# Query tiles outside, head pairs inside: the pair order of the odd mixer's sparse attention

## The chip, the core and the metric

One core of a Trainium2 chip runs one program: two transformer blocks of depth two, one after the other, in float32. The metric is the device time of one execution in microseconds. TensorE is called PE, VectorE DVE, ScalarE ACT, GpSimd POOL, SyncE SP, as in the profile.

## The reference, cut to what matters

The second block's odd layer has a mixer with eight query heads in two key groups over 512 tokens. Each head attends three times: to 31 compressed keys, to selected blocks of 64 keys, and to a window of 512 keys. With 512 tokens, 16 blocks are selected out of 8, and the window covers everything, so both large branches are plain causal attention with their own keys and values. Cut to its core:

```python
def masked_softmax(s, mask):
    return jax.nn.softmax(jnp.where(mask, s.astype(jnp.float32), NEG_INF), axis=-1)
...
        o_sel = jnp.einsum('bgmqkl,bgqkld->bgmqd', p, vs)
...
        s = jnp.einsum('bgmqd,bgsd->bgmqs', qb, kwb)
        o_win = jnp.einsum('bgmqs,bgsd->bgmqd', masked_softmax(s, win_ok).astype(vwb.dtype), vwb)
        o = jnp.stack([o_cmp, o_sel, o_win], axis=-1).reshape(b, NSA_HEADS, Q_BLOCK, d, 3)
        return jnp.einsum('bhqdc,bhqc->bqhd', o, gb)
```

After it the mixer computes a retention over the same tokens, from columns of the same input projection, and an output projection of both.

## The kernel before, in words

Every engine has one instruction queue, which it works off in the order written; semaphores tie the queues together. Nothing reorders the work at run time and no planner is used: the order is that of the Python loops.

**The work in pairs.** The attention runs over 16 *pairs* u = 0 to 15 (`NSA_PAIRS`, L1903): a pair is two neighbouring heads hp = (2hp, 2hp+1) and one tile qt of 128 queries. Each head of the pair is a *unit* i = 2u, 2u+1 (`NSA_UNITS`, L1904). A unit with tile qt sees (qt+1)*128 keys in each of the two branches. A pair has n = qt+1 *chunks* (`nsa_chunks`, L2163): a chunk is 128x512, two blocks of 128 keys by two heads. So there are four pairs with each of n = 1, 2, 3, 4, 32 units and 40 chunks, whatever the order. Before, the tile runs inside: n = 1, 2, 3, 4, 1, 2, 3, 4, ...

**The steps.** `nsa_order` (L2172) writes one list of steps, and PE, ACT and DVE each walk the same list:

- *scores* S(i): PE multiplies six times (L2204 to L2206: high part, causal mask, low part, for two branches) into two PSUM banks chosen by i % 2. DVE takes the row maxima (L2283). ACT takes the exponential of both branches (L2250). DVE inverts the sums (L2285), multiplies by the gate (L2288) and scales the first branch (L2291) while ACT scales the second (L2255). DVE stands still while ACT takes the exponentials, because the next instruction in its queue needs their sums.
- *turn* T(u,c): PE transposes the four 128x128 blocks of a chunk (L2215); ACT copies the high part to SBUF (L2262); DVE subtracts to get the low part (L2297).
- *values* V(u,c): PE multiplies the chunk with the values (L2228, L2229); with the last chunk of a pair the compressed branch is added (L2237, L2238), ACT copies half (L2269) and DVE adds the halves into the output (L2304). The last two are called O below.

**Their order.** The scores of pair u+1 are written ahead, inside pair u: one before its first turn and one before its second (or at the pair's end, where it has one chunk only). The values of a chunk are written behind the next turn. For a pair of n = 3 the list is S, T0, V(previous pair, last), S, T1, V0, T2, V1, and then the S of the pair after. The core of it:

```python
                for c in range(len(nsa_chunks(u))):
                    if ahead:
                        out.append(ahead.pop(0))
                    out.append(("turn", u, c))
                    if last:
                        out.append(("values",) + last)
                    last = (u, c)
                out += ahead
```

Buffers: four rows of probabilities (`nsa_row`, i % 4), three chunk buffers (`NPT`), two turn banks (4 and 5), two output banks (6 and 7), six sets of statistics.

**Around it.** Ahead of the stage stand the projections, the compression and the scores of the compressed branch. Behind it, on PE directly after the last values, stand the projections for the retention (`pe_odd_in(site, RET_IN)`) and `pe_retention`. At the mixer's end `act_retention` splits the eight 128-row chunks of the output; for chunk k < 4 it waits until the last attention result of head pair k is written (L2445). POOL and SP wait for the last pair of all (L2368, L2524), which is pair 15 with n = 4 in either order.

Of the kernel before, what the change touches and what calls it, by code (L numbers as in the profile page):

```python
# [32 lines left out]
TT = T2 // P  # L33
# [318 lines left out]
def build(nc, dram, out, book):  # L352

    with ExitStack() as ctx:
# [24 lines left out]
        def signal(name, step=1):  # L379
            s = Signal(ctx.enter_context(nc.semaphore(name)), name, book, step)  # L380
            signals[name] = s
            return s
# [6 lines left out]
        pe, act, dve, pool, sp = (Queue() for _ in range(5))  # L389
# [26 lines left out]
        scaled = signal("scaled")  # L416
# [9 lines left out]
        added = signal("added")  # L426
# [52 lines left out]
        def h_part(k, a, b):  # L479
            return HS[:, 0, k, a:b], HS[:, 1, k, a:b]  # L480
# [50 lines left out]
        def act_prepare():  # L531
            if act_next[0] == len(blocks):
                return
            key = blocks[act_next[0]]
            act_next[0] += 1
            _, nk, w = block_shape(*key)
            i = block_no[key]
            if i >= N_SLOTS and book:
                act.wait_ge(product, *book["ended"][blocks[i - N_SLOTS]])
            act.wait_ge(raw_in[raw_slot(key)], *key)  # L540
            act.e.activation(ws[:, i % N_SLOTS, 0, 0:nk * w], raw_view(key), ACT.Copy).then_inc(*w_hi(*key))  # L541
# [1030 lines left out]
        def act_evict(key, dst, func=ACT.Copy, cols=slice(0, T2), **more):  # L1572
            act.wait_ge(product, *key)
            act.e.activation(dst, banks.at(*key)[:, cols], func, **more).then_inc(*banks.back(key, copied, *key))  # L1574
# [325 lines left out]
        ROPED_N = ["kc", "ks", "kw", "q0", "q1", "q2", "q3"]  # L1900
        ROPED_R = [c[0] for c in RET_IN[:8]]
        ROPED = ROPED_N + ROPED_R
        NSA_PAIRS = [(hp, qt) for hp in range(4) for qt in range(TT)]  # L1903
        NSA_UNITS = [(2 * hp + a, qt) for hp, qt in NSA_PAIRS for a in range(2)]  # L1904
        nsa_scale = NSA_D ** -0.5

# [256 lines left out]
        def nsa_chunks(u):  # L2163

            nt = NSA_PAIRS[u][1] + 1
            tiles = [(br, kt) for br in range(2) for kt in range(nt)]
            return [tiles[2 * c:2 * c + 2] for c in range(nt)]

        chunk_list = [(u, c) for u in range(len(NSA_PAIRS)) for c in range(NSA_PAIRS[u][1] + 1)]
        chunk_no = {key: n for n, key in enumerate(chunk_list)}  # L2170

        def nsa_order():  # L2172

            out = [("scores", 0), ("scores", 1)]
            last = None
            for u in range(len(NSA_PAIRS)):
                ahead = [("scores", i) for i in (2 * u + 2, 2 * u + 3) if i < len(NSA_UNITS)]
# [13 lines left out]
        def pe_nsa():  # L2191
# [4 lines left out]
            for what, *at in nsa_order():  # L2196
# [21 lines left out]
                else:  # L2218
                    u, c = at
                    hp, qt = NSA_PAIRS[u]  # L2220
                    g, n = hp // 2, len(nsa_chunks(u))
# [50 lines left out]
        def dve_nsa():  # L2272
            for what, *at in nsa_order():
# [25 lines left out]
                elif at[1] == len(nsa_chunks(at[0])) - 1:  # L2299
                    u = at[0]  # L2300
                    hp, qt = NSA_PAIRS[u]
                    dve.wait_ge(copied, "nsa_o", u)
# [17 lines left out]
        def act_odd(site):  # L2320
            act_odd_in(KEYS_IN)
            act_keys()
            act_odd_in(Q_IN)
            act.wait_ge(con2_in)
            act.e.activation(ident_r, ident, ACT.Copy).then_inc(*halved("ident"))
            act.e.activation(causal_r, k2("causal"), ACT.Copy).then_inc(*halved("causal"))
            for c in range(4):
                act_queries(c)
            act_compress()
            act_cmp()  # L2330
            act_cmp_turn()
            act_nsa()
            act_odd_in(RET_IN)
            act_retention()
# [84 lines left out]
        def act_retention():  # L2419
            for what, h in RET_ORDER:  # L2420
                x = h % 2
                if what == "g":
                    if x == 0:
                        act_prepare()
                    act_evict(("ret_g", h), RG[:, h, :], ACT.Silu)
                elif what == "o":
                    if h > 1:
                        act.wait_ge(scaled, "ret", h - 2)
                    act_evict(("ret_o", h), RO[x])
                elif what == "mean":  # L2430
                    sq = rows.take(act, "ret", h)
                    act.wait_ge(conv, "ret", h)
                    act.e.activation(sq, RO[x], ACT.Square).then_inc(*squared("ret", h))
                elif what == "var":
                    r = rstd[:, x, :]
                    if h > 1:
                        act.wait_ge(added, "ret", h - 2)
                    act.wait_ge(product, "ret_var", h)
                    act.wait_ge(filled, "eps5")
                    act.e.activation(r, banks.at("ret_var", h), ACT.Ln, bias=eps5, scale=1.0 / P).then_inc(  # L2440
                        *banks.back(("ret_var", h), logged, "ret", h))
                    act.wait_ge(logged, "ret", h)
                    act.e.activation(r, r, ACT.Exp, scale=-0.5).then_inc(*rooted("ret", h))
            for k in range(DC):
                act.wait_ge(*((scaled, "nsa_o", 4 * k + 3, 1) if k < 4 else (added, "ret", k - 4)))  # L2445
                act.e.activation(h_part(k, *ALL)[0], OY[:, k, :], ACT.Copy).then_inc(*h_hi("od_y", ALL, k))

        def dve_retention():
# [359 lines left out]
```

## Time and profile before

| | before |
|---|---|
| median of 3 runs | 4115.38 us (4113.83 to 4117.14) |
| profiled execution, its time | 4118.89 us |
| profiled execution, its span | 4117.2 us |
| PE matmul busy | 3743.1 us, 91% |
| DVE busy | 1827.8 us, 44% |
| ACT busy | 1417.2 us, 34% |
| POOL busy | 473.5 us, 12% |
| mean granted clock of PE | 0.942 |
| the attention stage (first row maximum to the end of the last output add) | 3354.56 to 3518.52 us of the span |

Engine lines of the page give the busy time of each engine; the timeline gives single instructions with the idle time before each one and what ended it. PEclk is the granted clock as a share of 2.4 GHz, so 0.50 is 1.2 GHz and 1.00 is 2.4 GHz.

### The profile page before, as it was taken

The page shows a single profiled execution, that of the slowest core. Times are in us where ns is not written, and L with a number is a line of the kernel's source. Part 1 is how long each engine was busy: PE and PEld are TensorE (multiplying, and loading weights), DVE is VectorE, ACT ScalarE, POOL GpSimd, SP SyncE. Part 2 cuts the span into 40 slices and gives each one's busy share as a digit, 9 for nine tenths or more (in the row PEclk, how much of TensorE's full clock was granted, in tenths as well). Part 3 has the DMA queues.
Part 4 walks back from the last instruction along what each step waited for, and adds up shares of the span by engine and source line. Part 5 has one row for each costly group of instructions (what it writes and reads, how often), then busy time and mean ns, then how long its engine had stood idle before and what let it go on. Part 6 is the DMA issues. An engine that isn't in the chain of part 4 may idle for free.

```text
span 4117.2 us, 43513 instructions
## 1 busy us (share of the span) xinstructions
PE 3743.1 (91%) x18338; PEld 2954.1 (72%) x18338; DVE 1827.8 (44%) x2504; ACT 1417.2 (34%) x2153; POOL 473.5 (12%) x324
## 2 busy tenths in 40 slices
PE   7788988998999998899999999878999877988997
PEld 5555766777888886567766788666888666766886
DVE  5588544114543533664422545444433455324233
ACT  4344345113432324333322423334222344243222
POOL 0133100112100110110012101112000210221001
PEclk9889988999999999999999999989999877999999
DMA  4222100111112111220112222211232200212222
GB/s 180 72 91 85 57 26 31 46 67 42 62 57 72 62 57 63 80 98 32 46 61 82 78 98 93 96 62 64 90 110 87 85 21 1 82 52 72 90 97 70
DMA packets 55044, 289.85 MB, mean 70 GB/s; under 512 B 6977, under 2 KB 14401, under 8 KB 28737
## 3 DMA queue, kind: packets, MB, share of 16 engines
q1 hardware_dynamic: 54848, 287.06, 20.5%
q8 instruction: 145, 2.38, 0.2%
q14 instruction: 51, 0.41, 0.0%
HBM read 284.94 MB, written 2.10 MB: 70 GB/s over the span
## 4 chain that ended last, share of the span: by engine, by line
PE 79%; DVE 10%; ACT 6%; issue 2%; POOL 2%; DMA 1%; SPq 1%; POOLq 0%; ACTq 0%; DVEq 0%
PE psum L587 21%; PE psum L588 21%; PE psum L589 21%; PE psum L579 12%; DVE arena L1148 1%; POOL arena L1559 1%; ACT arena L1059 1%; PE psum L1011 1%; DVE arena L1176 1%; ACT arena L2250 1%; PE psum L886 1%; DVE arena L1160 1%; DVE arena L777 1%; DVE arena L1205 1%; DVE split_inputs L784 1%
## 5 line engine op out<-in xcount | busy, mean ns | idle before, releaser
L587 PE MATMUL psum<-split_inputs,split_weights 128*128 128x512 f32 (+2 forms) x3080 | 1170.4, 380 | 87.3 <-DVE split_inputs L784 33.8
L588 PE MATMUL psum<-split_inputs,split_weights 128*128 128x512 f32 (+2 forms) x3080 | 1136.1, 369 | 0.0
L589 PE MATMUL psum<-split_inputs,split_weights 128*128 128x512 f32 (+2 forms) x3080 | 1134.9, 368 | 0.0
L579 PE MATMUL psum<-arena 128*64 128x128 f32 (+14 forms) x3104 | 713.0, 397 | 111.8 <-DVE arena L1176 65.9
L587 PEld LDWEIGHTS psum<-split_inputs,split_weights 128*128 128x128 f32 (+1 forms) x3080 | 587.5, 191 | 227.7 <-issue 83.6
L579 PEld LDWEIGHTS psum<-arena 128*128 128x128 f32 (+4 forms) x3104 | 439.7, 189 | 367.8 <-issue 220.7
L588 PEld LDWEIGHTS psum<-split_inputs,split_weights 128*128 128x128 f32 (+1 forms) x3080 | 589.2, 191 | 101.0 <-issue 10.8
L589 PEld LDWEIGHTS psum<-split_inputs,split_weights 128*128 128x128 f32 (+1 forms) x3080 | 587.8, 191 | 97.3
L552 DVE TENSOR_TENSOR split_weights<-arena,split_weights 128x2048 fp32r<-128x2048 f32 (+1 forms) x228 | 472.8, 2074 | 396.7 <-ACT split_weights L541 396.5
L541 ACT ACTIVATE split_weights<-arena 128x2048 fp32r<-128x2048 f32 (+1 forms) x228 | 387.5, 1699 | 128.4 <-PE psum L589 121.5
L587 PE MATMUL psum<-split_hidden,split_weights 128*128 128x512 f32 (+1 forms) x880 | 324.0, 368 | 0.0
L588 PE MATMUL psum<-split_hidden,split_weights 128*128 128x512 f32 (+1 forms) x880 | 323.9, 368 | 0.0
L589 PE MATMUL psum<-split_hidden,split_weights 128*128 128x512 f32 (+1 forms) x880 | 323.7, 368 | 0.0
L1059 ACT ACTIVATE arena<-psum,arena 128x768 f32<-128x768 f32 (+1 forms) x160 | 130.9, 818 | 262.6 <-DVE arena L1151 253.2
L1574 ACT ACTIVATE arena<-psum 128x512 f32<-128x512 f32 (+2 forms) x128 | 71.6, 559 | 403.5 <-PE psum L589 398.7
L1216 POOL TENSOR_TENSOR arena<-arena 128x1024 f32<-128x1024 f32 x64 | 128.0, 2000 | 619.6 <-DVE arena L1205 374.2
L587 PEld LDWEIGHTS psum<-split_hidden,split_weights 128*128 128x128 f32 x880 | 165.9, 189 | 28.3 <-DVE split_weights L552 0.8
L589 PEld LDWEIGHTS psum<-split_hidden,split_weights 128*128 128x128 f32 x880 | 165.9, 188 | 27.7
L588 PEld LDWEIGHTS psum<-split_hidden,split_weights 128*128 128x128 f32 x880 | 165.9, 189 | 27.5
L619 POOL TENSOR_TENSOR arena<-arena 128x512 f32<-128x512 f32 (+1 forms) x60 | 71.2, 1186 | 960.7 <-ACT arena L596 960.7
L596 ACT ACTIVATE arena<-arena 128x512 f32<-128x512 f32 (+1 forms) x135 | 79.1, 587 | 292.0 <-DVE arena L1455 102.2
L1405 ACT ACTIVATE arena<-psum,arena 128x512 f32<-128x512 f32 (+1 forms) x132 | 92.3, 702 | 220.6 <-PE psum L589 220.5
(239 smaller groups left out, 4030.1 us busy)
## 6 DMA issues: line engine op xcount, KB each, us to landing
arena<-w_ada_dram SPq DMA_DIRECT2D x48, 1024.0 KB, 4.9
arena<-w_up_dram SPq DMA_DIRECT2D x44, 1024.0 KB, 4.9
arena<-ffn_up_dram SPq DMA_DIRECT2D x44, 1024.0 KB, 4.8
arena<-w_in_dram SPq DMA_DIRECT2D x28, 1024.0 KB, 4.9
arena<-w_down_dram SPq DMA_DIRECT2D x32, 704.0 KB, 4.1
arena<-ffn_down_dram SPq DMA_DIRECT2D x32, 704.0 KB, 4.1
arena<-od_w_in_dram SPq DMA_DIRECT2D x13, 1024.0 KB, 4.9
arena<-w_br_dram SPq DMA_DIRECT2D x16, 512.0 KB, 3.6
```

Source lines behind the costliest of these rows:

```text
L541: act.e.activation(ws[:, i % N_SLOTS, 0, 0:nk * w], raw_view(key), ACT.Copy).then_inc(*w_hi(*key))
L552: dve.e.tensor_tensor(ws[:, i, 1, 0:nk * w], raw_view(key), ws[:, i, 0, 0:nk * w].bitcast(F32), ALU.subtract).then_inc(*w_lo(*key))
L579: ins = pe.e.matmul(dst, a, b, start=i == 0, stop=i == n - 1)
L587: pe.e.matmul(dst, a[0], b[0], start=i == 0, stop=False)
L588: pe.e.matmul(dst, a[0], b[1], start=False, stop=False)
L589: ins = pe.e.matmul(dst, a[1], b[0], start=False, stop=i == n - 1)
L596: act.e.activation(row, view, ACT.Square).then_inc(*squared(site, s, c))
L619: pool.e.tensor_tensor(acc, acc, rows.at(site, s, c)[:, 0:w], ALU.add).then_inc(*rows.back((site, s, c), pooled, site, s, c))
L1059: act.e.activation(score_rows(u, sub)[:, 0:u["keys"]], psum[:, b * BANK:b * BANK + u["keys"]], ACT.Exp, bias=st[:, 3 * sub + 1:3 * sub + 2 ...
L1216: pool.e.tensor_tensor(wt[:, j, :], wt[:, j, :], wide[:, s, :], ALU.mult).then_inc(*multiplied(al, b, j))
L1405: act.e.activation(y, banks.at("up", l, half, m, s, g)[:, 0:n], ACT.Identity, bias=vc(l, "conv_b", ch), scale=vc(l, "conv_w", 2 * FC + ch) ...
L1574: act.e.activation(dst, banks.at(*key)[:, cols], func, **more).then_inc(*banks.back(key, copied, *key))
```

## The change

The two loops in the list of pairs are exchanged. Pairs now come as n = 1, 1, 1, 1, 2, 2, 2, 2, 3, 3, 3, 3, 4, 4, 4, 4, with the head pair running inside. The wait of `act_retention` for "all four tiles of head pair k" used the number 4k+3 of the pair (k, 3), which has another number now; it is looked up.

```diff
-        NSA_PAIRS = [(hp, qt) for hp in range(4) for qt in range(TT)]
+        NSA_PAIRS = [(hp, qt) for qt in range(TT) for hp in range(4)]
...
-                act.wait_ge(*((scaled, "nsa_o", 4 * k + 3, 1) if k < 4 else (added, "ret", k - 4)))
+                act.wait_ge(*((scaled, "nsa_o", NSA_PAIRS.index((k, TT - 1)), 1) if k < 4 else (added, "ret", k - 4)))
```

Every instruction of the stage is there as before, with the same shapes; what changes is which of them stand next to each other in the five queues. No DMA is issued inside the stage in either order.

## Rows read from the trace of the kernel before

**Rows 1.** Stretches: start:end, us, busy and instructions by engine, PEclk, DMA share, GB/s.

```profile
3354.56:3518.52 163.96, 113.50 (x543) 96.35 (x543) 83.05 (x201) 81.08 (x217) 0.10 (x1) 0.72 0.00 1
```

**Rows 2.** Waits of DVE in the stage: total us, times, longest us.

```profile
DVE arena L2285 <- ACT arena L2250: 38.2, 32, 1.5
...
DVE arena L2283 <- PE psum L2206: 9.0, 8, 2.0
```

**Rows 3.** Timeline, DVE: start us, us, engine, line, operation, [idle before <-releaser].

```profile
3356.45 0.42 DVE L2283 TENSOR_REDUCE arena<-psum 128x2 f32<-128x256 f32 x1
...
3358.34 0.68 DVE L2283 TENSOR_REDUCE arena<-psum 128x2 f32<-128x512 f32 x1
...
3387.31 0.42 DVE L2283 TENSOR_REDUCE arena<-psum 128x2 f32<-128x256 f32 x1 [1.96 <-PE psum L2206]
...
3390.53 0.59 DVE L2304 TENSOR_TENSOR arena<-psum,arena 64x128 f32<-64x128 f32 x2
...
3398.05 0.69 DVE L2283 TENSOR_REDUCE arena<-psum 128x2 f32<-128x512 f32 x1 [0.82 <-PE psum L2206]
...
3401.86 0.59 DVE L2304 TENSOR_TENSOR arena<-psum,arena 64x128 f32<-64x128 f32 x2
...
3402.48 0.69 DVE L2283 TENSOR_REDUCE arena<-psum 128x2 f32<-128x512 f32 x1
...
3404.92 0.95 DVE L2283 TENSOR_REDUCE arena<-psum 128x2 f32<-128x768 f32 x1
...
3409.32 0.59 DVE L2304 TENSOR_TENSOR arena<-psum,arena 64x128 f32<-64x128 f32 x2
...
3414.33 1.22 DVE L2283 TENSOR_REDUCE arena<-psum 128x2 f32<-128x1024 f32 x1
...
3419.31 0.59 DVE L2304 TENSOR_TENSOR arena<-psum,arena 64x128 f32<-64x128 f32 x2
...
3431.49 0.42 DVE L2283 TENSOR_REDUCE arena<-psum 128x2 f32<-128x256 f32 x1
```

**Rows 4.** Timeline, DVE, ends of four-chunk pairs and the last three-chunk pair.

```profile
3396.53 0.69 DVE L2297 TENSOR_TENSOR split_low<-psum,split_low 128x512 fp32r<-128x512 f32 x1 [1.48 <-ACT split_low L2262]
...
3437.65 0.69 DVE L2297 TENSOR_TENSOR split_low<-psum,split_low 128x512 fp32r<-128x512 f32 x1 [2.26 <-ACT split_low L2262]
...
3439.16 0.69 DVE L2283 TENSOR_REDUCE arena<-psum 128x2 f32<-128x512 f32 x1 [0.82 <-PE psum L2206]
...
3510.59 0.69 DVE L2297 TENSOR_TENSOR split_low<-psum,split_low 128x512 fp32r<-128x512 f32 x1 [2.27 <-ACT split_low L2262]
```

**Rows 5.** Timeline, PE, inside the stage, same columns.

```profile
3358.69 1.09 PE L2215 MATMUL psum<-arena 128*128 128x128 f32 x4 [1.51 <-ACT arena L2255]
...
3408.60 0.52 PE L2204 MATMUL psum<-split_high 128*128 128x384 f32 x1
...
3409.45 1.06 PE L2215 MATMUL psum<-arena 128*128 128x128 f32 x4
...
3411.16 0.63 PE L2204 MATMUL psum<-split_high 128*128 128x512 f32 x1
...
3412.22 0.53 PE L2204 MATMUL psum<-split_high 128*128 128x512 f32 x1
...
3427.24 1.07 PE L2215 MATMUL psum<-arena 128*128 128x128 f32 x4
...
3434.84 0.58 PE L2228 MATMUL psum<-split_high 128*128 128x256 f32 x1 [0.89 <-DVE split_high L2297]
...
3435.86 1.05 PE L2215 MATMUL psum<-arena 128*128 128x128 f32 x4
...
3437.57 0.41 PE L2204 MATMUL psum<-split_high 128*128 128x256 f32 x1
```

**Rows 6.** Stretches again: a chunk end inside the stage, and the work after it.

```profile
3425.00:3427.50 2.50, 2.46 (x12) 2.46 (x13) 0.59 (x1) 0.00 (x0) 0.00 (x0) 0.50 0.00 0
...
3512.00:3560.00 48.00, 46.45 (x205) 36.31 (x204) 18.76 (x16) 13.01 (x14) 13.02 (x11) 1.00 0.26 88
```

## The prediction, made before the changed kernel was run

> **What bounds the kernel now.** First the busy shares (the table above): PE is busy 91% of the span, so outside this stage the kernel is matmul work. Then the stretch of the attention stage: 163.96 us, 4.0% of the span, in which PE is busy for 113.50, DVE for 83.05, ACT for 81.08, and the granted clock averages 0.72 [rows 1]. No engine fills it, so a chain through several engines sets its length. The list of DVE's waits names the chain: 38.2 us in 32 waits, one in each unit, are DVE standing at L2285 for ACT's exponentials [rows 2]. DVE's queue is in order, so a unit costs DVE the whole round trip of maxima, exponentials, inverses and scaling, with nothing beside it. The timeline of DVE then gives the cost of each kind of step and shows where DVE waits for PE besides [rows 3, 4].
>
> The steps as DVE's queue passes them. A unit of one block with nothing behind it: 3358.34 - 3356.45 = 1.89 us; of two blocks: 3404.92 - 3402.48 = 2.44. A unit followed by a turn, from its maxima to the output add behind that turn: 3.22 (one block, 3390.53 - 3387.31), 3.81 (two, 3401.86 - 3398.05), 4.40 (three, 3409.32 - 3404.92), 4.98 (four, 3419.31 - 3414.33). An output add O: 0.62 (3402.48 - 3401.86) [rows 3]. So one block more costs a unit about 0.57 us.
>
> **The change, part by part.**
>
> *The steady chain.* All 32 units and 40 turns stay in DVE's queue, and the list puts a unit beside a turn as often as before (26 units have a turn behind them, 6 have none). Only which lengths stand alone changes: before 2 units of one block and 4 of two; after 5 of one and 1 of two. Followed units were 6, 4, 8, 8 of one to four blocks and become 3, 7, 8, 8. By the costs above this is 3 x 1.89 - 3 x 2.44 - 3 x 3.22 + 3 x 3.81 = +0.1 us. The hope that a long softmax now stands beside a long turn finds nothing here: DVE hides neither under the other.
>
> *The waits for PE.* These are what can move. Before:
> - After a pair of n = 3: DVE has done its last turn and waits 1.96 us for the next pair's scores (at 3387.31, three of these in all) [rows 3]. PE's order there is V1, then the scores, and V1 waits for DVE's low part of T1. After it PE needs V1 (1.02 us, 3434.84 to 3435.86 [rows 5]) and six score matmuls, while DVE has one turn of 0.61 left.
> - After a pair of n = 4: a turn waits 1.48 or 2.26 (one and two times) and the scores behind it 0.82 (three of these) [rows 4], for the same reason, one turn later.
> - The last pair of n = 3 is followed by the last pair, which has no scores ahead: 2.27 (at 3510.59) [rows 4].
> - The maxima waited 9.0 us in 8 times [rows 2]: 3 x 1.96, 3 x 0.82, and 0.7 in two small ones.
> Together 9.0 + (1.48 + 2.26 + 2.26) + 2.3 = 17.3 us. This waiting doesn't come from unequal neighbours but from the order V, S at a pair's end. Both orders have it, at the same number of pairs; what changes is how large the scores are that DVE waits for. Before, they were the smallest (one block after n = 3, two after n = 4); now they are of three or four blocks.
>
> *Size of the scores.* At the low clock half of a unit's scores takes PE 3409.45 - 3408.60 = 0.85 us with three blocks and 3412.22 - 3411.16 = 1.06 with four [rows 5]: +0.21 per block and half, +0.42 per unit. With two blocks, start to DVE's maxima is 3439.16 - 3437.57 = 1.59 [rows 4, 5]; so I take 2.01 for three and 2.43 for four. With one block the weight loads keep it near 1.5.
>
> *After, all at the low clock.*
> - n = 3: the scores waited for have three blocks twice (into pairs 10 and 11) and four blocks twice (12 and 13): 1.96 + 0.5 = 2.5 and 1.96 + 0.95 = 2.9; 2 x 2.5 + 2 x 2.9 = 10.8.
> - n = 4: the turn waits 2.26 three times, 6.8. The scores behind have four blocks and now occur twice: 0.82 + 0.84 = 1.66 each, 3.3.
> - Into the last pair, now behind n = 4: its first turn is transposed right behind V2, so that PE's part is V1, T3, V2, T0. With 1.02 + 1.7 (T3 and V2, 3435.86 to 3437.57) + 1.07 for the transposes, then ACT's copy of 0.6, I get some 4.5 us from T1's end, when DVE has come to 3.5: a wait of 1.0 in place of 2.27.
> - n = 1, new: three pairs of n = 1 in a row. From the second unit's maxima to PE's transposes 3358.69 - 3356.45 = 2.24, from the transposes over V and S to the next maxima 3431.49 - 3427.24 = 4.25 [rows 3, 5]: 6.49 us per pair by way of PE, against 1.89 + 3.22 + 0.62 = 5.73 by DVE. Here PE is late: 0.76 for each of pairs 1 and 2, about 0.2 for pair 3 (its units ahead have two blocks), 1.7 in all. Pair 0 has no V before it.
> - n = 2: DVE needs 2 x 3.81 + 0.62 = 8.2 us, PE at the low clock about 7.1 (two scores of 1.28, from the half of 0.85 less 0.21; twice 1.7 for a turn with its V; 1.0 more for the V with the compressed branch, since 4.25 - 1.59 - 1.7 leaves 1.0; all from [rows 4, 5]): no wait. A turn before the next turn costs DVE what it did.
> Sum: 10.8 + 6.8 + 3.3 + 1.0 + 1.7 + 0.1 = 23.7 us, against 17.3: +6.4.
>
> *The clock.* The price of each of these waits hangs on PE's clock at that place. Before, the two and a half microseconds behind a chunk's end ran at 0.50 [rows 6], since PE had stood idle for DVE ahead of them; of the seven pair ends one (3396.53, waiting 1.48 and not 2.26 [rows 4]) had part of its work at the high clock. If every pair end ran at the high clock, PE's parts would halve and ACT's and DVE's stay: waits of about 1.2 and 1.4 after n = 3, 1.4 and 0.35 after n = 4, 0.3 into the last pair, none at n = 1. That is 2 x 1.2 + 2 x 1.4 + 3 x 1.4 + 2 x 0.35 + 0.3 + 0.1 = 10.5 us, or -6.8. These are the two ends, +6.4 and -6.8. I take the low clock for six pair ends in seven, as the rows show it: 6.4 - 13.2 / 7 = +4.5.
> The Trainium skill ("TensorE: Matmul & The Clock Gate", Part 1) says that idleness throttles the array and sustained activity releases it. By that rule the pairs of n = 1 and 2, where PE has hardly a gap, would run at the high clock and lose the 1.7 us, for +2.8. The rows don't bear it out for short stretches: PE was busy in 2.46 of the 2.50 us from 3425.0 at clock 0.50 [rows 6], and its four transposes right behind, at 3427.24, still took 1.07 us [rows 5].
>
> *Everything else at nothing.* L2445 waits for results that are finished tens of microseconds before, with RET_IN between. POOL and SP wait for pair 15, the last in both orders. No DMA is in the stage (DMA share 0.00 [rows 1]), so none can be pushed. The output is written tile by tile instead of head by head, but nothing reads it before the retention is over. PE's projections follow the last V directly, and PE stands at clock 1.00 from 3512 on [rows 6].
>
> The profiled execution took 4118.89 us, 3.5 above the median of the runs; with +4.5 it would be 4123.4, and the median 4119.9. I forecast **4119.9 us**.
>
> **The rivals.**
> - *High clock at the pair ends.* Priced above: -6.8, 4108.6 us. For it: in the three-block pairs DVE's unit, for which PE stands idle before V1, is 4.40 and not 4.98 us long [rows 3], and PE's own scores are longer than the one-block ones in the old four-block pairs. Against: the four-block pairs keep the long idle time, and all three n = 3 ends before were low.
> - *Low clock throughout and into the projections.* The four-block pairs at the end leave PE idle for microseconds in each of their long units; if it comes to the projections at 0.50 and not at 1.00, every microsecond of them at half speed costs half a microsecond. A low stretch of 7 us past the last V costs 3.5, with +6.4 it is +9.9: 4125.3 us. It decides from the moment the clock is still low at the last V. Against: the turns and values of the last pair run close together, and before they raised the clock, from the same steps.
> - *Equal neighbours hide each other.* If the waits came from a short pair covering a long softmax, they would go: -17.3, 4098.1 us. Against it stands the place of the waits, which is behind V1, and not before a long unit.
>
> **How the numbers follow.** The forecast's case has 0.63, the high clock 0.14, the low clock into the projections 0.17, equal neighbours 0.06. About 0.2% (8.2 us) is what a measurement of this kernel can tell from no change. Faster than 4107.2: nearly all of the last case and a fifth of the high-clock case, 0.08. Slower than 4123.6: most of the third case and the forecast's upper edge, 0.17. The same: 0.75. For the range: below, the high clock (4108.6) with most of its chance inside or near 4110; above, 4125.3 and a little for a low stretch longer than 7 us, 4126.5.
>
> **What would show it.** The stage should last about 168.5 us. The first four pairs: DVE waits below 1 us for scores. The second four: none. The third four: each ends with maxima waiting for L2206, 2.4 to 3. The last three but one: a turn waiting about 2.3, then maxima about 1.7. Into the last pair: a turn waiting about 1. DVE's 32 waits for the exponentials should sum to 38 us again. I am wrong if these 38 us shrink, if DVE waits in the two-chunk pairs, or if the stage is outside 155 to 172 us.

## The result and the profile after

The changed kernel is slower by about a quarter of a percent. In the first timing its median is 4128.06 us (4126.86 to 4130.79, 6 runs) against 4116.26 (4112.47 to 4121.47, 6 runs): ratio 1.0028, 95% interval 1.0015 to 1.0041. Timed again beside 33 runs of before it is 1.0022 (1.0013 to 1.0031). The forecast was 4119.9 in a range to 4126.5: the time lies outside it, on the side that had 0.17. Each ratio is against runs of before from its own timing, and those bases differ by up to 6 us, which matters below.

The page's first lines (span; busy time, share and instructions of each engine): the same instructions in number, 7.9 us more of span.

```profile
span 4125.1 us, 43513 instructions
...
PE 3750.7 (91%) x18338; PEld 2958.2 (72%) x18338; DVE 1829.8 (44%) x2504; ACT 1416.2 (34%) x2153; POOL 470.8 (11%) x324
```

The stretch of the stage, from the first row maximum to the end of the last output add (columns as in [rows 1]):

```profile
3357.04:3526.34 169.30, 117.62 (x543) 99.15 (x543) 83.24 (x201) 80.94 (x217) 0.10 (x1) 0.69 0.00 1
```

It is 169.30 us, 5.3 more than in [rows 1], and PE's clock there is 0.69 and not 0.72. Two more profiles of the changed kernel give 169.31 and 169.75, two more of before 162.86 and 162.91: mean 169.5 against 163.2, **+6.2 us**. The waits of DVE in the stage, as in [rows 2]:

```profile
DVE arena L2285 <- ACT arena L2250: 38.2, 32, 1.5
...
DVE arena L2283 <- PE psum L2206: 15.1, 10, 2.9
```

The round trips to ACT are 38.2 us again, to the tenth. What grew is maxima waiting for PE, from 9.0 to 15.1 us. The timeline of DVE shows where (start, duration, instruction, idle before it and its releaser), first the row of one-chunk pairs, then the ends of the three-chunk pairs, then those of the four-chunk pairs, and last the first turn of pair 15:

```profile
3370.45 0.42 DVE L2283 TENSOR_REDUCE arena<-psum 128x2 f32<-128x256 f32 x1 [0.46 <-PE psum L2206]
...
3376.94 0.42 DVE L2283 TENSOR_REDUCE arena<-psum 128x2 f32<-128x256 f32 x1 [0.53 <-PE psum L2206]
...
3383.55 0.69 DVE L2283 TENSOR_REDUCE arena<-psum 128x2 f32<-128x512 f32 x1 [0.32 <-PE psum L2206]
...
3432.94 0.96 DVE L2283 TENSOR_REDUCE arena<-psum 128x2 f32<-128x768 f32 x1 [2.49 <-PE psum L2206]
...
3445.39 0.96 DVE L2283 TENSOR_REDUCE arena<-psum 128x2 f32<-128x768 f32 x1 [2.36 <-PE psum L2206]
...
3458.41 1.23 DVE L2283 TENSOR_REDUCE arena<-psum 128x2 f32<-128x1024 f32 x1 [2.92 <-PE psum L2206]
...
3472.59 1.22 DVE L2283 TENSOR_REDUCE arena<-psum 128x2 f32<-128x1024 f32 x1 [2.92 <-PE psum L2206]
...
3486.11 0.69 DVE L2297 TENSOR_TENSOR split_low<-psum,split_low 128x512 fp32r<-128x512 f32 x1 [2.27 <-ACT split_low L2262]
...
3487.91 1.22 DVE L2283 TENSOR_REDUCE arena<-psum 128x2 f32<-128x1024 f32 x1 [1.11 <-PE psum L2206]
...
3501.44 0.69 DVE L2297 TENSOR_TENSOR split_low<-psum,split_low 128x512 fp32r<-128x512 f32 x1 [2.26 <-ACT split_low L2262]
...
3503.80 1.23 DVE L2283 TENSOR_REDUCE arena<-psum 128x2 f32<-128x1024 f32 x1 [1.67 <-PE psum L2206]
...
3518.82 0.69 DVE L2297 TENSOR_TENSOR split_low<-psum,split_low 128x512 fp32r<-128x512 f32 x1 [0.81 <-ACT split_low L2262]
```

Four waits of 2.36 to 2.92 us stand where [rows 3] had three of 1.96. They wait for L2206, the last score matmul. PE at the first of them (same columns):

```profile
3429.91 0.58 PE L2228 MATMUL psum<-split_low,split_high 128*128 128x256 f32 x1 [3.49 <-DVE split_low L2297]
...
3430.93 0.52 PE L2204 MATMUL psum<-split_high 128*128 128x384 f32 x1
...
3432.63 1.05 PE L2215 MATMUL psum<-arena 128*128 128x128 f32 x4
```

PE had been idle for DVE's low part; then it does V1 in 1.02 us and the six score matmuls in 1.7 to the next start, and DVE waits for both. The clock there (stretches, PEclk the third number from the end):

```profile
3430.30:3432.90 2.60, 2.60 (x12) 2.52 (x11) 0.15 (x1) 0.00 (x0) 0.00 (x0) 0.50 0.03 6
3442.90:3445.30 2.40, 2.40 (x12) 2.32 (x11) 0.13 (x1) 0.00 (x0) 0.00 (x0) 0.50 0.00 0
3455.30:3458.40 3.10, 3.10 (x12) 2.63 (x12) 0.18 (x1) 0.00 (x0) 0.00 (x0) 0.50 0.00 0
```

It is 0.50 at each of these, as in [rows 6]. In the row of one-chunk pairs it is 0.50 as well:

```profile
3357.00:3372.00 15.00, 11.46 (x50) 10.33 (x49) 7.45 (x28) 8.20 (x32) 0.00 (x0) 0.50 0.00 1
```

One DMA is issued inside the stretch, in both orders: SP's load of the decays, when the last pair's product is done, about 1 us before the stage ends. It changes nothing in the account.

### The profile page after: what moved, and what is told of

It is laid out like the page before. It is cut to its first block, busy times and chain, and to the rows that moved or that the text cites. A ratio compares the mean times of both kernels' runs of the same rounds, so it can differ in the third digit from the quotient of the medians.

```text
span 4125.1 us, 43513 instructions
## 1 busy us (share of the span) xinstructions
PE 3750.7 (91%) x18338; PEld 2958.2 (72%) x18338; DVE 1829.8 (44%) x2504; ACT 1416.2 (34%) x2153; POOL 470.8 (11%) x324
## 4 chain that ended last, share of the span: by engine, by line
PE 79%; DVE 10%; ACT 6%; issue 2%; POOL 2%; DMA 1%; SPq 1%; ACTq 0%; POOLq 0%; DVEq 0%
PE psum L587 21%; PE psum L588 21%; PE psum L589 21%; PE psum L579 12%; DVE arena L1148 1%; POOL arena L1559 1%; ACT arena L1059 1%; PE psum L1011 1%; DVE arena L1176 1%; ACT arena L2250 1%; PE psum L886 1%; DVE arena L1205 1%; DVE arena L1160 1%; DVE arena L777 1%; DVE arena L2283 1%
## 5 line engine op out<-in xcount | busy, mean ns | idle before, releaser
L588 PEld LDWEIGHTS psum<-split_inputs,split_weights 128*128 128x128 f32 (+1 forms) x3080 | 588.1, 191 | 100.9 <-issue 10.8
```

The costliest lines, as they stand in the source:

```text
L588: pe.e.matmul(dst, a[0], b[1], start=False, stop=False)
```

## The experiments

**The two kernels again.** No edit.

> The kernel before, unchanged, as its own control. Ratio 1.000 within 0.1%; attention stage 164 us (first row maximum to last output add) within 2 us. If the rest of the measured +11.8 us beyond the stage's +5.6 is only where the free clock steps fell in the first 700 us, this profile will stand some us off the first one there too, and its stage will not. If instead the stage itself differs from run to run by several us, the stage will show it.

Measured: 0.9999 (0.9990 to 1.0008), 4118.45 us. Its stage:

```profile
3361.24:3524.10 162.86, 111.92 (x543) 94.76 (x543) 82.91 (x201) 81.10 (x217) 0.10 (x1) 0.71 0.00 1
```

The stage is 1.1 us shorter than in the first profile, but the execution longer by 5.7: the stage begins at 3361.24 and not 3354.56. The 598.7 us behind it are the same. DVE waits 7.8 us for maxima here and in the profile below, not 9.0: the two-block scores behind four chunks wait 0.50 us, 0.33 us and not at all, where each waited 0.82 in the first profile. So executions of one kernel differ mostly ahead of the stage; over all runs of before they lie between 4111.6 and 4126.9 us.

> The changed kernel, unchanged, a second time. Theory (larger scores behind V1 at pair ends, and pairs of one chunk in a row): stage 169 to 171 us again with the same waits, maxima waiting 2.4, 2.4, 2.9, 2.9 us after the three-chunk pairs; total +5 to +8 us against before. Rival (something outside the stage is slower by 6 us too): stage 170 us again but total +12 us, and a stretch outside the stage that is longer in both profiles of the changed kernel than in both of before.

Measured: 1.0022 (1.0013 to 1.0031), 4128.39 us; stage 169.31, beginning at 3355.82, 599.2 behind it. The waits are those of the first profile:

```profile
DVE arena L2285 <- ACT arena L2250: 38.2, 32, 1.5
...
DVE arena L2283 <- PE psum L2206: 15.0, 10, 2.9
```

> A third profile of the kernel before. Two are there: stage 163.96 and 162.86 us, beginning at 3354.6 and 3361.2; the rest behind it 598.6 us in both. Theory (what differs between executions is the time ahead of the stage, where both kernels run the same instructions): the stage again 162 to 165 us, the rest 598.6, and the beginning anywhere from 3350 to 3362. Rival (the stage of the old order has fast executions of its own): a stage under 161 us.

Measured: one run, 4122.55 us; stage 162.91, beginning at 3359.22, 598.7 behind it.

> A third profile of the changed kernel: stage 169.3 us as in the two there are, the rest 599; beginning 3350 to 3362. If the beginning never falls below 3355.8 in the changed kernel while it does in the old one, the times beyond the stage's +5.9 us are not chance.

Measured: one run, 4130.77 us; stage 169.75, beginning at 3360.65, 598.6 behind it. In the six profiles the stage alone separates the kernels clearly; its beginning is 3354.6 to 3361.2 in the one and 3355.8 to 3360.7 in the other, and what follows it differs by 0.6 us at most. The test set above, whether the changed kernel ever begins below 3355.8, is too fine for this: it does not, and before does once of three times, by 1.3 us. The interval of 1.0022 is +5.4 to +12.8 us on 4120, and +6.2 lies in it. That all of the 9 us is the stage is not shown; no other stretch was found that holds the rest. Within the stage DVE's waits hold it all: those for maxima grow from 8.2 to 15.2 us in the mean of three profiles each, and those of the turns fall from 28.1 to 27.2.

**The next pair's scores ahead of V.** All three engines walk the changed list, but ACT and DVE have nothing to do at a V that is not a pair's last, so only PE's order changes.

```diff
-            return out + [("values",) + last]
+            out.append(("values",) + last)
+            for j in range(1, len(out)):
+                if out[j][0] == "scores" and out[j][1] % 2 == 0 and out[j - 1][0] == "values":
+                    out[j - 1], out[j] = out[j], out[j - 1]
+            return out
```

> The changed kernel with one swap on each pair's end: the first scores of the pair after stand ahead of V(n-2) in the list, not behind it. Only PE's order changes. Theory (V1 holds up the scores): the four waits of maxima after three-chunk pairs, 10.7 us, go to nearly 0; behind four-chunk pairs the turn still waits 2.3 and the maxima fall from 1.1 and 1.7 to about 0.7; stage about 157.5 us, 12 us below the changed kernel's. Rival (the waits are PE's slow clock or the exponentials, not the order of V and S): the waits stay within 1 us of what they were, stage 167 to 170 us.

Measured: 0.9986 (0.9977 to 0.9995), 4116.26 us; stage 158.9, 10.6 below the changed kernel. The timeline of DVE, the end of the first three-chunk pair and of a four-chunk pair (L2287 are the maxima, L2301 the turns here):

```profile
3431.49 0.68 DVE L2301 TENSOR_TENSOR split_high<-psum,split_high 128x512 fp32r<-128x512 f32 x1
...
3432.09 0.95 DVE L2287 TENSOR_REDUCE arena<-psum 128x2 f32<-128x768 f32 x1
...
3476.77 0.69 DVE L2301 TENSOR_TENSOR split_low<-psum,split_low 128x512 fp32r<-128x512 f32 x1 [2.26 <-ACT split_low L2266]
...
3478.28 1.23 DVE L2287 TENSOR_REDUCE arena<-psum 128x2 f32<-128x1024 f32 x1 [0.82 <-PE psum L2210]
```

The maxima at 3432.09 follow the turn at once, where they had waited 2.5 us, and none of the four waits behind three-chunk pairs is left; behind four chunks the turn still waits 2.26, as expected, for it needs T1's low part and V1. The stage is 1.4 us longer than the 157.5 expected. This is the theory's own prediction, and its rival (waits within 1 us) falls. PE shows the order at work: the last score matmul is over before V1 has stopped waiting.

```profile
3429.02 0.38 PE L2210 MATMUL psum<-split_high 128*128 128x384 f32 x1
3431.63 0.58 PE L2232 MATMUL psum<-split_low,split_high 128*128 128x256 f32 x1 [2.22 <-DVE split_low L2301]
```

These scores ran at the high clock, but that alone doesn't take the wait away: with V1 still ahead of them and the clock at 1.00, the filled kernel below waits 1.25 us.

> The same swap in the kernel before (tile inside). Theory: its 3 x 1.96 and 3 x 0.82 us of maxima waiting go, stage about 156 us, 8 us below before; and with this swap the two loop orders differ by under 3 us, since what told them apart was the size of the scores behind V1. Rival (the loop order costs through the row of one-chunk pairs or the clock): the two swapped kernels still differ by 6 us or more.

Measured: 0.9978 (0.9970 to 0.9987), 4112.04 us; stage 155.0, 8.2 below before. Maxima waiting for PE:

```profile
DVE arena L2287 <- PE psum L2210: 1.3, 4, 0.5
```

They fall from 9.0 (7.8 in the later profiles) to 1.3 us. The two orders now differ by 3.9 us of stage and not 6.2; I had said under 3, and the rival 6 or more, so neither was met. The largest part of the 3.9 is the clock at the ends of four-chunk pairs. There the turn waits 1.36, 1.36 and 1.37 us in this kernel, and 2.26, 2.26 and 2.25 in the swapped kernel with the new order, 2.7 us more. The stretch before the first of these turns, here and then in the other kernel:

```profile
3393.50:3396.00 2.50, 1.98 (x17) 1.98 (x18) 1.14 (x3) 0.87 (x2) 0.00 (x0) 0.96 0.03 7
...
3474.00:3476.70 2.70, 2.70 (x11) 2.60 (x12) 0.51 (x1) 0.56 (x1) 0.00 (x0) 0.50 0.00 0
```

The maxima make 1.9 us (3.2 against 1.3: the row of one-chunk pairs, and four-block scores behind four-chunk pairs, still 0.8 each), and output adds take 0.6 off. One profile of each was taken, so it is open whether the loop order or chance sets the clock at these ends.

**Matmuls that keep PE busy ahead of V1.** Their results are read by nobody.

```diff
+                    if c == 1 and n > 2 and 2 * u + 2 < len(NSA_UNITS):
+                        pe.wait_ge(exped, "nsa", 2 * u + 2, 0)
+                        for _ in range((12, 18)[n - 3]):
+                            pe.e.matmul(banks.views[0][:, 0:2 * P], NV[:, 0, 2 + g, :], NKK[:, 0, 0:2 * P],
+                                        start=True, stop=True)
                     pe.wait_ge(taken, "nsa", u, c)
```

> The changed kernel with 12 (three chunks) or 18 (four) idle-time matmuls of 256 columns ahead of V1, into a score bank whose contents are used up; their results are read by nobody. They fill the time in which PE waits for DVE, so that the clock should stand at 1.00 at the pair ends. Theory of the price (PE's part of each pair-end wait doubles at 0.50): with the clock at 1.00 the maxima wait 1.2 to 1.4 us and not 2.4 to 2.9, the turns 1.4 and not 2.3; stage about 161 to 163 us. Where the clock stays at 0.50 in spite of them, the fill takes 12 x 0.21 = 2.6 us or 18 x 0.21 = 3.8 us and may itself delay V1 by up to 1 us. Rival (the clock is not what sets these waits): stage 169 us or more with the clock at 1.00 there.

Measured: 0.9995 (0.9985 to 1.0004), 4120.42 us; stage 163.6, just above the 161 to 163 expected and 6 us less than without them, with more work on PE. The maxima behind the first and the third of the three-chunk pairs:

```profile
3435.44 0.96 DVE L2288 TENSOR_REDUCE arena<-psum 128x2 f32<-128x768 f32 x1 [1.25 <-PE psum L2206]
...
3459.16 1.23 DVE L2288 TENSOR_REDUCE arena<-psum 128x2 f32<-128x1024 f32 x1 [2.28 <-PE psum L2206]
```

and the clock in these stretches:

```profile
3432.80:3435.40 2.60, 1.75 (x13) 1.73 (x14) 1.29 (x2) 0.56 (x2) 0.00 (x0) 1.00 0.00 0
3456.00:3459.10 3.10, 2.76 (x12) 2.33 (x13) 0.89 (x2) 0.05 (x1) 0.00 (x0) 0.68 0.03 5
```

With the clock at 1.00 the wait is 1.25 us (2.49 without them); where a stretch at 1.2 GHz falls into the end, 0.68, it is 2.28 (2.92). The clock is at 1.00 at two of the four ends, and both wait 1.25; at the other two it is 0.68 and 0.65, and they wait 2.28 and 2.18. Two of the three turns fall to 1.38 us, one stays at 2.26. So where the clock was high, half of the pair-end wait went, as the working had it: 1.2 was its figure for three blocks. For four blocks at the high clock (1.4) there is no case.

**An order between the two.**

```diff
-        NSA_PAIRS = [(hp, qt) for qt in range(TT) for hp in range(4)]
+        NSA_PAIRS = [(hp, 0) for hp in range(4)] + [(hp, qt) for hp in range(4) for qt in range(1, TT)]
```

> The four one-chunk pairs first, then n = 2, 3, 4 for each head pair. By the terms found so far (size of the scores waited for, and the row of one-chunk pairs): row of one-chunk pairs 2.0; behind three chunks the scores now have two blocks, 3 x 2.05 = 6.2; behind four chunks the turn 3 x 2.26 = 6.8 and scores of three blocks 3 x 1.24 = 3.7; into the last pair 2.27; together 21.0 us against 23.1 in the changed kernel: stage 167.3 us, between the two orders (163.2 and 169.5). Rival (it is the equal neighbours, or the clock over the whole stage): the stage equals the old order's within 1 us, or the new one's.

Measured: 1.0008 (0.9999 to 1.0017), 4124.17 us; stage 165.5, between the two as expected, but 1.8 below the figure. The end of a three-chunk pair and of a four-chunk pair:

```profile
3409.72 0.69 DVE L2283 TENSOR_REDUCE arena<-psum 128x2 f32<-128x512 f32 x1 [2.07 <-PE psum L2206]
...
3420.01 0.69 DVE L2297 TENSOR_TENSOR split_low<-psum,split_low 128x512 fp32r<-128x512 f32 x1 [1.37 <-ACT split_low L2262]
...
3421.68 0.96 DVE L2283 TENSOR_REDUCE arena<-psum 128x2 f32<-128x768 f32 x1 [0.98 <-PE psum L2206]
```

The two-block scores wait 2.07, 2.07 and 2.06 us, 6.2 as summed. With 1.96 for one block, 2.49 for three and 2.92 for four, all at clock 0.50, this is the step by size. The four-chunk ends are short: turns 1.37, 1.61 and 2.26 (5.2, not 6.8) and maxima 0.98, 1.24 and 0.63 (2.9, not 3.7). The terms of size hold; I had priced every end at the low clock, and these stood partly at the high one (clock 0.91 in the 3 us before the turn at 3420.01).

**V two turns behind.** In both orders; the next pair's first scores also go ahead of the last turn on PE.

```diff
-                    if last:
-                        out.append(("values",) + last)
-                    last = (u, c)
+                    last.append((u, c))
+                    if len(last) > 2:
+                        out.append(("values",) + last.pop(0))
                 out += ahead
-            return out + [("values",) + last]
+            return out + [("values",) + at for at in last]
...
+                if len(nsa_chunks(u)) > 2:
+                    scores = ("scores", 2 * u + 4)
+                    out.remove(scores)
+                    out.insert(out.index(("turn", u, len(nsa_chunks(u)) - 1)), scores)
```

> The old loop order with V two turns behind instead of one, and the next pair's first scores on PE ahead of the pair's last turn. Theory: no V at a pair's end waits by itself any more, scores are ready early; of the 17.3 us of waits only about 1.2 us before the last turn of each four-chunk pair is left, and the tail; stage about 151 to 154 us, total 10 to 12 us below before, 2 to 4 below the kernel with the swap alone. Rival (PE at the low clock or the tail takes it back): stage 155 us or more.

Measured: 0.9973 (0.9964 to 0.9982), 4111.40 us. The stage, and the last turn of the first four-chunk pair:

```profile
3358.73:3510.69 151.96, 114.39 (x543) 98.79 (x543) 82.49 (x201) 81.81 (x217) 0.10 (x1) 0.69 0.01 1
...
3398.26 0.69 DVE L2307 TENSOR_TENSOR split_low<-psum,split_low 128x512 fp32r<-128x512 f32 x1 [1.18 <-ACT split_low L2272]
```

> The new loop order with V two turns behind and the next pair's first scores ahead of the last turn (as in the kernel with a stage of 151.96 us in the old order). Theory: the size of the scores no longer costs anything, since none stands behind a V that waits; what is left of the loop order's price is the row of one-chunk pairs, about 2 us: stage 153 to 155 us, total 2 us above the old order with the same edit, about 9 us below before. Rival (a cost of the order that is not in the terms): stage 157 us or more.

Measured: 0.9970 (0.9960 to 0.9980), 4106.80 us. The stage, and the last turn of a four-chunk pair:

```profile
3353.51:3502.93 149.42, 105.63 (x543) 91.08 (x543) 82.54 (x201) 81.83 (x217) 0.10 (x1) 0.76 0.00 1
...
3468.87 0.69 DVE L2307 TENSOR_TENSOR split_low<-psum,split_low 128x512 fp32r<-128x512 f32 x1 [0.21 <-ACT split_low L2272]
```

The expectation of 153 to 155 fell: 149.42 us, and the new order is now the shorter. The turns that wait 1.18, 1.38 and 1.48 us in the old order wait 0.21, 0.28 and 0.67 here. PE ahead of the turn at 3468.87 (L2214 is the first score matmul, L2225 the transposes):

```profile
3463.49 0.39 PE L2214 MATMUL psum<-split_high 128*128 128x512 f32 x1
...
3467.48 0.66 PE L2225 MATMUL psum<-arena 128*128 128x128 f32 x4 [2.70 <-DVE split_low L2307]
```

PE has the four-block scores of the next pair behind it by 3464.8 and waits for DVE, which is in a four-block unit; then its transposes take 0.66 us, at the high clock. In the old order a four-chunk pair has one-block units beside it, DVE is through soon, and PE has no gap before the turn at 3398.26, though part of its work there runs at the high clock:

```profile
3395.70:3398.20 2.50, 2.50 (x19) 2.50 (x18) 1.31 (x4) 1.03 (x2) 0.00 (x0) 0.74 0.03 7
```

Neighbours and clock move together in these two kernels (stage means 0.69 and 0.76); the repetition below has a case that parts them.

> Old order with V two turns behind, again: stage 151 to 153 us, the turns before the last of each four-chunk pair waiting 1.2 to 1.5 us; total 10 to 12 us below before.

Measured: 0.9971 (0.9960 to 0.9982), 4111.33 us (7 runs, one of them at 4097.81, the others 4109.05 to 4113.05); stage 150.6, just below the expected 151 to 153; the turns wait 1.26, 1.44 and 1.52.

> New order with the same edit, again. If the 149.42 us seen was the order's doing (long units of DVE beside PE's long turns, so that PE has caught up and stands at the high clock when the last turn comes), the stage is 149 to 150 us again, with waits below 0.4 us at those turns, 2 to 3 us below the old order with the edit in the stage and in the total. If it was a lucky placing of the clock's steps, it is 151 to 154 us.

Measured: 0.9970 (0.9958 to 0.9981), 4108.98 us; stage 149.8. The stage is in the expected place, but the turns wait 0.67, 0.21 and 0.67, so two of the three miss the 0.4, and the stage is 0.8 us below the old order's, not 2 to 3. In the two pairs of profiles it differs by 2.5 and 0.8 us, both times the same way, and these turns wait 1.2 us in the new order against 4.0 in the old, then 1.6 against 4.2; the row of one-chunk pairs and the last pair take part of that back. The first of the turns has PE's transposes at the low clock (1.12 us, not 0.66), and PE had stood idle before them all the same:

```profile
3471.83 1.12 PE L2225 MATMUL psum<-arena 128*128 128x128 f32 x4 [2.68 <-DVE split_low L2307]
...
3473.67 0.69 DVE L2307 TENSOR_TENSOR split_low<-psum,split_low 128x512 fp32r<-128x512 f32 x1 [0.67 <-ACT split_low L2272]
```

So with its transposes at the low clock the turn waits 0.67 us in the new order, against 1.18 to 1.52 in the old, where one of them even had part of the work at the high clock: the neighbours count by themselves, and the clock makes the difference between 0.67 and 0.21. Once no V stands in between, a long unit of DVE does cover PE's work for a long pair. In total the two intervals cover each other, so between these two no winner is timed. Both beat before by 0.3% and the changed kernel by 0.5%.

## Why the prediction was wrong

**The mechanism and the waits at the low clock were right.** Predicted waits, and those of the first profile after:

| | predicted | measured |
|---|---|---|
| maxima behind three chunks | 10.8 | 2.49 + 2.36 + 2.92 + 2.92 = 10.7 |
| turn in four-chunk pairs | 6.8 | 2.27 + 2.26 + 2.26 = 6.8 |
| maxima behind four chunks | 3.3 | 1.11 + 1.67 = 2.8 |
| first turn of pair 15 | 1.0 | 0.8 |
| row of one-chunk pairs | 1.7 | 0.46 + 0.53 + 0.32 and 2 x 0.18 = 1.7, and 0.3 one pair on |
| round trips to ACT | 38 | 38.2 |

The signs to look for came: no wait for scores above 0.3 us among the second four pairs, a stage inside 155 to 172. The swap showed that V1 is what the scores wait behind, the intermediate order that their size counts, the filling matmuls that the high clock halves the wait. One sum of the working is slightly off and bears on nothing: PE's time for a two-chunk pair adds up to 7.0 and not 7.1 us.

**The step that failed is the last one, "it would be 4123.4, and the median 4119.9".** The sum was put on the median of three runs, 4115.38 us, and the range was made of rivals alone, with no term for how well three runs know the base. Medians of before are 4116.26 (6 runs, beside the first timing), 4119.97 (33), 4122.42 (19), 4121.97 (18) and 4121.80 (12); over these 88 runs it is 4121.3, with single runs from 4111.6 to 4126.9. The profiled execution, at 4118.89 above all three runs, was the hint, and the step down by 3.5 us threw it away. From a base of 4121.3 the same +4.5 gives 4125.8, still 2.3 below the measured 4128.06.

**The term mis-sized is the clock's.** "I take the low clock for six pair ends in seven" took 1.9 us off. The count was near: in the first profile after, two of the seven ends stood partly at the high clock (0.74 at the wait of 1.11, 0.69 into the last pair). The price was not: the waits of the table together are only 0.8 us below their low-clock figures, for the 1.9 taken off.

**The miss in parts.** Of the 8.2 us between 4119.9 and 4128.06 the base makes 5.9, and the stage, +6.2 in place of +4.5, makes 1.7; about 0.6 is left. Set against the bases timed beside it, the changed kernel is 9 us slower (1.0022), or 11.8 in the first timing, whose base is low, and of these the stage's 6.2 is all that was located. That the undiscounted +6.4 lies so near to +6.2 is in part luck: the waits after are 0.8 us less than summed, and the later profiles of before have a stage 1.1 us shorter than the one that the sum was taken from. The first profile of each gives +5.3.

**The rivals.** The time lies where "slower" had 0.17, but not by the way that this chance was given for: the low clock into the projections did not come, and the stretch behind the stage is 599 us in both. The high clock at the pair ends did not come by itself in this kernel, but for parts of two; forced, it gave what it was priced at for three blocks (1.25 for 1.2) and for two of the turns (1.38 for 1.4). That the pairs of n = 1 and 2 would run at the high clock and lose the 1.7 us did not come either: the clock was 0.50 in the row of one-chunk pairs, which cost its 1.7 us. Equal neighbours didn't hide each other in this kernel, as the prediction said. DVE's own steps never hid each other in any of the kernels, the round trips staying at 38.2 us; but with V two turns behind, long units of DVE cover long turns of PE, and the new order has the shorter stage.

## What to carry to other kernels

When loops are exchanged in a software-pipelined stage, list which waits exist in both orders and what each one waits *for*: the count of waits may stay, while the thing waited for gets larger. Here a consumer that waits (V) stood ahead of an independent producer (the next scores) in one in-order queue; moving the producer ahead of it gave more (8 and 11 us of stage) than the loop order cost (6 us). With V two turns behind, the loop order's price was gone. And take the base of a forecast from many runs, with a term in the range for what the base may be off, before working out single microseconds.

## What the runs showed of the hardware that was not expected

Executions of one kernel differ by up to 15 us, with all instructions the same: the 33 runs of before timed on one chip lie between 4111.6 and 4126.8. Between the first two profiles of before, the 6.7 us of difference arose ahead of the stage: the granted clock over the first 700 us was 0.89 and 0.88, and between 700 us and the stage 0.97 and 0.96. Matmuls that compute nothing useful made the stage 6 us shorter: PE came out of its waits at 1.00 at two of the pair ends and at about 0.65 at others, instead of 0.50.
